# Low parts of the refilled token operands: both halves made on VectorE in every phase behind the head

## The reference, cut to what matters

```python
h = rmsnorm(x, g_pre[layer])
proj = jnp.einsum('btd,de->bte', h, w_in[layer])
(q_a, k_a, v_a, lr_a, z_a, q_b, k_b, v_b, z_b, m_a, m_b) = split_cols(proj)
...
o_a = rmsnorm(o_a, g_gla[layer]).reshape(B, T, GLA_V).astype(x.dtype) * jax.nn.silu(z_a)
y_a = jnp.einsum('bte,ed->btd', o_a, w_branch_gla[layer])
...
o_b = o_b.reshape(B, T, SWA_Q).astype(x.dtype) * jax.nn.silu(z_b)
y_b = jnp.einsum('bte,ed->btd', o_b, w_branch_swa[layer])
gate_a = jax.nn.sigmoid(m_a + b_merge[layer, :D_MODEL])
gate_b = jax.nn.sigmoid(m_b + b_merge[layer, D_MODEL:])
y = gate_a * y_a + gate_b * y_b
out = jnp.einsum('btd,de->bte', y, w_out[layer])
x = x + rmsnorm(out, g_post[layer])
```

## Time and profile before

| | us |
|---|---|
| median of 3 runs | 1956.26 |
| lowest, highest | 1953.11, 1956.53 |
| the profiled execution: its time | 1951.45 |
| the profiled execution: its span | 1949.6 |

### The profile page before, as it was taken

One profiled execution on the slowest core, in us unless ns is written; L12 is line 12 of the kernel. 1 busy time (PEld: TensorE's weight loads), 2 busy tenths in 40 slices (PEclk: granted clock), 3 DMA queues, 4 the chain that ended last, 5 costly groups with the idle time before them and its releaser, 6 DMA issues. The chain is left out here.

```text
span 1949.6 us, 28906 instructions
## 1 busy us (share of the span) xinstructions
PE 1911.5 (98%) x9972; PEld 1533.0 (79%) x9972; DVE 1239.7 (64%) x2069; ACT 844.6 (43%) x1893; POOL 987.4 (51%) x667
## 2 busy tenths in 40 slices
PE   8999999999999999999999999999999999999996
PEld 7878877777777777888888787877777777788885
DVE  6868876977776667623154888768577675763104
ACT  5466474543444443324333664544433444432221
POOL 4643455555433357643563445557654333775444
PEclk9999999999999999999999999999999999999998
DMA  7524375667667677745433334457767666775612
GB/s 277 157 73 135 107 243 185 198 216 228 203 193 238 214 241 254 237 140 197 138 120 108 102 115 162 154 182 241 229 192 233 214 220 218 275 249 162 196 42 87
DMA packets 255140, 359.42 MB, mean 184 GB/s; under 512 B 31059, under 2 KB 156563, under 8 KB 242195
## 3 DMA queue, kind: packets, MB, share of 16 engines
q1 hardware_dynamic: 254995, 357.57, 56.9%
HBM read 237.50 MB, written 120.00 MB: 183 GB/s over the span
## 5 line engine op out<-in xcount | busy, mean ns | idle before, releaser
L878 PE MATMUL pu<-a_hi,w_hi 128*128 128x512 f32 x1740 | 688.8, 398 | 10.3 <-DVE u L1769 6.4
L878 PE MATMUL pu<-a_hi,w_lo 128*128 128x512 f32 x1740 | 674.6, 390 | 0.5 <-POOL w_lo L1888 0.5
L878 PE MATMUL pu<-a_lo,w_hi 128*128 128x512 f32 x1740 | 673.7, 390 | 0.0
L1888 POOL TENSOR_TENSOR w_lo<-t,w_hi 128x512 fp32r<-128x512 f32 x244 | 347.7, 1431 | 402.7 <-ACT w_hi L1222 402.6
L1888 POOL TENSOR_TENSOR w_lo<-w_raw,w_hi 128x512 fp32r<-128x512 f32 x267 | 378.9, 1429 | 254.5 <-ACT w_hi L1222 254.5
L878 PEld LDWEIGHTS pu<-a_hi,w_hi 128*128 128x128 f32 x1740 | 326.5, 188 | 94.2 <-issue 26.3
L878 PEld LDWEIGHTS pu<-a_hi,w_lo 128*128 128x128 f32 x1740 | 326.6, 188 | 70.6 <-POOL w_lo L1888 0.9
L878 PEld LDWEIGHTS pu<-a_lo,w_hi 128*128 128x128 f32 x1740 | 327.0, 188 | 63.6
L879 PE MATMUL pu<-a_hi,w_hi 128*128 128x512 f32 x640 | 249.2, 389 | 0.0
L879 PE MATMUL pu<-a_lo,w_hi 128*128 128x512 f32 x640 | 249.0, 389 | 0.0
L879 PE MATMUL pu<-a_hi,w_lo 128*128 128x512 f32 x640 | 249.0, 389 | 0.0
(11 more groups left out here) (183 smaller groups left out, 2476.3 us busy)
## 6 DMA issues: line engine op xcount, KB each, us to landing
w_raw<-in_w SPq DMA_DIRECT2D x81, 1024.0 KB, 7.0
va_d<-ct SPq DMA_DIRECT2D x32, 256.0 KB
qb_d<-ct SPq DMA_DIRECT2D x32, 256.0 KB
zb_d<-ct SPq DMA_DIRECT2D x32, 256.0 KB
q_s<-qb_d SPq DMA_DIRECT2D x32, 256.0 KB, 3.8
z_s<-zb_d SPq DMA_DIRECT2D x32, 256.0 KB, 3.1
gb_d<-gb SPq DMA_DIRECT2D x32, 256.0 KB, 3.6
za_d<-ct SPq DMA_DIRECT2D x32, 256.0 KB
```

The source lines that it names most:

```text
L878: return nc.tensor.matmul(dst, weights, moving, start=start, stop=stop, skip_group_check=True)
L1888: TT(flat(w_lo[o.n % NWB][:, :, :]), src, as_f32(flat(w_hi[o.n % NWB][:, :, :])), ALU.subtract) \
```

## The change

`low_on_vector` decides which fills have their second low half made on VectorE. Before, these were the 7 `h` fills between the superblocks. Now it is every fill behind the head, which adds 8 `gb` and 4 `ga` fills per superblock, 24 in all.

```diff
 def low_on_vector(f):
 
-    return f.what == "h" and f.sb > 0
+    return f.n >= NHEAD
```

## The result

| | before | after |
|---|---|---|
| median us (7 runs each) | 1954.33 | 1960.68 |
| lowest to highest us | 1953.11 to 1958.12 | 1959.21 to 1962.00 |
| profiled execution: time, span | 1951.45, 1949.6 | 1962.00, 1960.2 |
| mean granted TensorE clock, profiled | 0.996 | 0.992 |

The ratio after to before is 1.0027, with a 95% interval of 1.0017 to 1.0036: 5.3 us slower (3.3 to 7.0). The forecast was 3.4 us faster, and the time lies above the range. The two profiled executions are 10.6 us apart: the one before is faster than all of its seven runs, the one after is the slowest of its own.

What follows compares the result with a forecast made beforehand. TensorE, busy 98% of the span, was taken as the bound, losing at most 3.95 us waiting for VectorE. Gains of 1.6, 1.4 and 0.4 us summed to -3.4 us, so 1952.9 us, range 1950.0 to 1958.0.

Steps and rivals of the forecast that it cites:

- What bounds the kernel, and exclusion by whole instructions: TensorE waits only for VectorE, 3.2 us in five waits; VectorE and GpSimd exclude each other an instruction at a time.
- First place, `mA` 3: Line 1780 at mA 3 starts 1.0 us earlier; the 0.7 us wait goes in both superblocks, 1.6 us gained.
- Queues: SyncE's next fill load moves by -1 to +1 us; stores and gate loads behind it have more slack than that.
- Second place, `yB` 1: The wait for line 1769 at yB 1 goes but for 0.2 us in each superblock, 1.4 us gained.
- The wait for line 1799: This 0.3 us wait goes because GpSimd's half of S1 no longer delays w_lo and the column sum: 0.4 us gained.
- The ga fills: 8 of the 24 halves, where TensorE shows no wait: no effect, at most the 0.5 us of one short wait.
- The slower one: Rival: w_lo falls between VectorE's halves, delaying lines 1780 and 1769 by 1.5 and 1.3 us: +5.6 us, chance 0.13.
- The no-gain one: Rival: S3's chain of loads slips by 1.5 us or more and yB 1 keeps its wait: 1954.7 to 1956 us, chance 0.2.

Runs made afterwards that it cites:

- a11_at_once: The full change, with only the second half of gb A11 made right behind its first half: ratio 0.9986 to the kernel before, 2.7 us faster.
- mixed_a11_late: gb_mixed with A11's second half a step later: ratio 1.0021 to the kernel before, where gb_mixed has 0.9966; 10.8 us between them.
- gb_sums: Against the kernel before, only the second halves of gb S1 to S4 moved to VectorE: ratio 0.9988, 2.3 us faster.
- gb_mixed_s2: gb_mixed with S2's second half also right behind its first: ratio 0.9975 to the kernel before, 4.9 us faster.
- gb_mixed: The full change with ga left on GpSimd and second halves of A11, A21, A22 right behind the first: 0.9966 to the kernel before, 6.6 us faster.
- loads_later: The full change with the loads of gb fills A21 and A22 one step later in SyncE's order: ratio 1.0017 to the kernel before, 3.3 us slower.

## Why the prediction was wrong

*What bounds the kernel, and exclusion by whole instructions: right.* Of the five waits three were the same to 0.1 us in three profiles of the kernel before (the wait for line 1799 is 0.2 to 0.6 us, that for line 1769 in superblock 1 is 0.5 to 1.0), and VectorE's busy time fell although it got 24 instructions.

*First place, `mA` 3: right.* Line 1780 starts 8.6 us behind line 1769 instead of 9.6, the 1.0 us that was forecast, and both waits of 0.7 us are gone in the full change.

*Queues: this is the step that failed.* "SyncE's next fill load waits for the later half; it moves by -1 to +1 us, and what stands behind it are stores and gate loads with more slack than that." It moved by +3.7 us, because the late half of A11 is put behind line 1776 a whole step on, and behind it stood `z_g`, which line 1718 needs. `a11_at_once` and `mixed_a11_late` show that the place of this one instruction is worth about 8 and 11 us by the times of the runs, 7 and 8 us by the stretch in the traces. I had taken the load's move from the operand's use five products on, and looked at the buffer only for S3.

*Second place, `yB` 1: right mechanism named as a rival, sizes wrong.* The forecast left 0.2 us of stall in each superblock; 3.4 and 2.3 us were measured. It had S3's first half 0.7 us later, a head start of 5.1 us, and a way of 3.5 or 4.75 us to line 1769. In superblock 0 the head start is 5.1 us, as forecast, and the way is 7.8 us: I allowed for one `w_lo` among VectorE's instructions and there were four. In superblock 1 the way is 5.7 us, with two `w_lo`, and the head start is 4.0 us. The number of `w_lo` doesn't follow from late fills: `gb_sums`, with fills in time, meets two, and `gb_mixed_s2`, with the half earlier still, meets four. What sets it is not shown; the forecast had no ground for one. `gb_sums` shows the added halves without late fills to cost nothing in the time.

*The wait for line 1799: wrong.* It was to go; it moved into `yB` 0 and is 0.7 us, from late S2.

*The ga fills: wrong.* "Nothing", or at most 0.5 us; it is a wait of 0.5 us and a loss of 0.7 to 0.8 us in each superblock, 1.5 us in all, where two halves and two `w_lo` stand in front of line 1780.

*The clock: not in the sum at all.* With a stall of 3.4 us went some 6.9 us at 1.2 GHz (about 1.2 of them still inside it), with one of 2.3 us 3.3 us. I counted 0.15 us of extra cost per stall.

*The rivals.* The slower one had the right end (+5.6 us), by luck: it counted 1.5 us at `mA` 3, where nothing was lost, and its 1.3 us at line 1769 doesn't come out of its own terms (749.81 + 3.5 + 2.5 = 755.8, 0.6 us later than before). The no-gain one named the chain of S3's loads, with 1.5 us as its point; the load slipped by 3.4. What happened is both together, and I had given them 0.13 and 0.2 apart. Nor did the order show me the price of a step: I read from it which instruction an added one stands in front of, and not which it stands behind.

*What stays open.* `gb_mixed` is 6.6 us faster, and its stretches are only 4.2 us shorter. That lies at the edge of the interval (4.1 to 9.2), and its runs' granted clock is 0.0007 higher in the mean, about 1.4 us. For `a11_at_once` the stretches and the `ga` fills give -0.3 us where -2.7 (-4.5 to -0.8) was measured. Both ran in the session in which the median of the kernel before was 1956.76, where the others have 1954.69 to 1955.16; whether that is the reason is not shown.

## What to carry to other kernels

When an instruction moves to another engine, find out first what it frees, a buffer or a semaphore that a DMA queue waits for, and how much later that comes; an operand's distance to its use says nothing about this. Put such an instruction directly behind what it needs, unless an eviction stands there, and count for every instruction of VectorE with two SBUF inputs one of GpSimd's in front of it when both queues are full. Ask of a stall both how long the way to the eviction is and how early it begins. Above all look at stalls that are already near 1 or 2 us: making one of them longer can cost the clock as well.

## What the runs showed of the hardware

An instruction of VectorE with two SBUF inputs and one of GpSimd alternated here whenever both had work in their queues: 1.22 us became 2.26 to 2.34, 0.68 became 1.75 to 1.78, four times in a row, and two of 1.22 us behind each other took 5.04. The eviction behind them, with one input in SBUF and one in PSUM, kept its length (line 1769: 0.65 to 0.69 us, 61 times in the kernel after).
The Trainium skill ("SBUF — State Buffer", section "Who interferes with whom") has this as an exclusive lock for a whole instruction, and by that rule the trace agrees; that a queue of them pays the other engine's instruction every time is what the rows add.

The granted clock fell with stalls of 3.36 and 2.31 us in the kernel after (to means of 0.77 and 0.89 over 15 us). At `yB` 0 and `yB` 1, over all profiles, it fell with all five stalls of 3.1 us or more, with five of the seven of 2.1 to 2.6 us (2.30 us in `loads_later` and 2.33 us in `mixed_a11_late` left it at 1.00), and with none of those up to 1.9 us. At the stall near 360 us, 2.3 us long in every version, it fell in 8 of the 17 profiles and not in the others (0.93 against 1.00 over 350 to 375 us, in two of the three profiles of the kernel before and not in the first). The spread of the times goes with the clock: executions of the kernel before with a mean clock of 0.996 have a median of 1953.6 us, those with 0.994 one of 1957.0 (18 and 20 of 84 executions).
